# Two recurrence turns per loop body, and another order of instructions at a turn's boundary, in a hybrid decoder step

## What is computed

```python
def step(S, inp):
    r_t, w_t, k_t, v_t, a_t, b_t = inp
    sa = jnp.einsum('nhvk,nhk->nhv', S, a_t)
    S = S * w_t[:, :, None, :] + sa[..., None] * b_t[:, :, None, :] + v_t[..., None] * k_t[:, :, None, :]
    return S, jnp.einsum('nhvk,nhk->nhv', S, r_t)
...
mean = jnp.mean(y, axis=-1, keepdims=True)
var = jnp.mean(jnp.square(y - mean), axis=-1, keepdims=True)
y = ((y - mean) * lax.rsqrt(var + LNX_EPS)).reshape(n, t, A_WIDTH) * lnx_w + lnx_b
bonus = jnp.sum(r * k * r_k.astype(f32), axis=-1, keepdims=True) * v
y = (y + bonus.reshape(n, t, A_WIDTH)) * jax.nn.silu(za.astype(f32))
```

## Time and profile before

| what | value |
|---|---|
| runs | 3548.31, 3549.05, 3569.71 us, median 3549.05 us |
| profiled execution | 3559.79 us, span of the core 3558.3 us |
| granted clock of TensorE, mean | 0.945 |
| TensorE matmul | 92% of the span |
| TensorE weight load | 85% |
| VectorE | 48% |
| ScalarE | 30% |
| GpSimd | 11% |

### The profile page before, as it was taken

The page is one execution under the profiler, slowest core; times in us unless marked ns, Lnnn a source line. Parts: engine busy times, 40 slices in busy tenths (PEclk is TensorE's granted clock), DMA queues, the critical chain, the costliest instruction groups (busy, mean ns, idle before and its releaser), DMA issues. The chain is left out here.

```text
span 3558.3 us, 82556 instructions
## 1 busy us (share of the span) xinstructions
PE 3279.7 (92%) x33471; PEld 3028.9 (85%) x33471; DVE 1721.4 (48%) x2447; ACT 1054.2 (30%) x1680; POOL 395.8 (11%) x795
## 2 busy tenths in 40 slices
PE   3899999999997899999999999999999999996796
PEld 3798898898994889988988998998989998895796
DVE  3254454354443445655654654654654654563324
ACT  3232232332320322332332332432332332331222
POOL 2100100100001201110110110110110110111000
PEclk6899898998995999999999999999999999998898
DMA  2222323323313212221221221311221221221422
GB/s 86 71 79 72 125 73 91 119 60 103 106 36 108 71 53 56 74 55 45 75 62 38 74 63 43 80 51 49 75 62 49 64 62 50 61 61 42 150 75 97
DMA packets 368508, 255.10 MB, mean 72 GB/s; under 512 B 19412, under 2 KB 347600, under 8 KB 366288
## 3 DMA queue, kind: packets, MB, share of 16 engines
q1 hardware_dynamic: 342592, 184.18, 18.9%
q0 software_dynamic: 25600, 66.02, 5.8%
HBM read 212.69 MB, written 37.45 MB: 70 GB/s over the span
## 5 line engine op out<-in xcount | busy, mean ns | idle before, releaser
L363 PE MATMUL psum<-act_hi,w_hi 128*128 128x280 f32 (+3 forms) x5216 | 1613.2, 309 | 89.8 <-DVE w_lo L349 38.7
L365 PE MATMUL psum<-act_hi,w_lo 128*128 128x280 f32 (+3 forms) x5216 | 1539.9, 295 | 0.0
L364 PE MATMUL psum<-act_lo,w_hi 128*128 128x280 f32 (+3 forms) x5216 | 1539.1, 295 | 0.0
L363 PEld LDWEIGHTS psum<-act_hi,w_hi 128*128 128x128 f32 (+2 forms) x5216 | 999.6, 192 | 162.7 <-issue 107.0
L364 PEld LDWEIGHTS psum<-act_lo,w_hi 128*128 128x128 f32 (+2 forms) x5216 | 999.0, 192 | 6.0 <-issue 1.0
L365 PEld LDWEIGHTS psum<-act_hi,w_lo 128*128 128x128 f32 (+2 forms) x5216 | 998.3, 191 | 1.1
L349 DVE TENSOR_TENSOR w_lo<-raw,w_hi 128x1024 fp32r<-128x1024 f32 (+1 forms) x326 | 396.6, 1217 | 320.9 <-ACT w_hi L341 306.4
L341 ACT CAST w_hi<-raw 128x1024 fp32r<-128x1024 f32 (+1 forms) x326 | 340.1, 1043 | 87.4 <-DMA raw<-in_w_in_dram 36.5
L1937 PE MATMUL psum<-arena 64*64 64x64 f32 x9216 | 309.4, 219 | 6.6 <-DVE arena L1782 6.5
L1937 PEld LDWEIGHTS psum<-arena 64*64 64x64 f32 x9216 | 286.1, 134 | 32.9 <-issue 32.9
L1497 POOL DMA_DIRECT2D out_s_rwkv_dram<-arena x128 | 78.9, 624 | 1558.5 <-ACT arena L1639 1558.4
(11 more groups left out here) (312 smaller groups left out, 3513.8 us busy)
## 6 DMA issues: line engine op xcount, KB each, us to landing
raw<-in_w_in_dram SPq DMA_DIRECT2D x288, 512.0 KB, 4.6
arena<-in_state_gla_dram POOLq DMA_DIRECT2D x32, 512.0 KB, 5.3
out_s_gla_dram<-arena POOLq DMA_DIRECT2D x32, 512.0 KB, 3.3
raw<-in_w_out_dram SPq DMA_DIRECT2D x32, 512.0 KB, 4.5
ob_dram<-arena POOLq DMA_DIRECT2D x16, 280.0 KB, 3.1
arena<-ob_dram POOLq DMA_DIRECT2D x16, 280.0 KB, 5.8
m_dram<-arena POOLq DMA_DIRECT2D x16, 280.0 KB, 2.4
arena<-m_dram SPq DMA_DIRECT2D x4, 1120.0 KB, 12.2
```

What stands on the lines that cost most here:

```text
L363: pe.matmul(out, hi, act_hi[:, k, cols], start=(k == 0), stop=False)
L364: pe.matmul(out, hi, act_lo[:, k, cols], start=False, stop=False)
L365: mm = pe.matmul(out, lo, act_hi[:, k, cols], start=False, stop=(k == KT - 1))
```

## The change

All five edits are in stage D.

1. In the programs of GpSimd, ScalarE, VectorE and TensorE the loop has 7 passes of two turns, and turn 14 is written out behind it, ahead of turn 15. SyncE's loop is as before.
2. TensorE transposes the sample states after 16 steps of tile 3. ScalarE copies them between its two halves of tile 3's tanh.
3. Tile 4's tanh and its multiplication are taken in halves inside the doubling rounds: ScalarE's first half after its copy of round 1, VectorE's first half after its addition of round 2.
4. At the end of a turn TensorE takes the mean before the products of the sample states, and the variance 8 steps behind those, before the states are transposed. ScalarE splits tile 7 before it copies the results, and evacuates tile 6 and splits tile 8 behind the roots.
5. VectorE centres first, then splits tile 7 and computes the sample states; its split of tile 8 and its key shift come last in the turn.

```diff
-                with pool.Fori(0, LAST_TURN) as i:
-                    turn_of(i)
+                with pool.Fori(0, LAST_TURN // 2) as j:
+                    turn_of(2 * j)
+                    turn_of(2 * j + 1)
+                turn_of(LAST_TURN - 1)
                 turn_of(LAST_TURN, last=True)
...  (the same in the programs of ScalarE, VectorE and TensorE)
                 # ScalarE
-                    tanh_gate_of(3, tg)
-
+                    tanh_gate_of(3, tg, (0,))
                     act.wait_ge(s8_turned.sem, s8_turned.at(i, 1))
                     nc.scalar.copy(s8, bank[6].rearrange("p (s v) -> p s v", s=NSEQ)).then_inc(s8_ready.sem, 1)
                     act.wait_ge(s8_ready.sem, s8_ready.next(i))
+                    tanh_gate_of(3, tg, (1,))
...
                         to_sbuf(out, 6, inv_a)
-                    tanh_gate_of(4, tg)
+                        if n == 1:
+                            tanh_gate_of(4, tg, (0,))
+                    tanh_gate_of(4, tg, (1,))
...
                     tanh_gate_of(5, tg)
+                    if not last:
+                        pd.split_hi(act, i, mine, 7)
                     act.wait_ge(y_state.sem, y_state.at(i, 1))
...
-                    if not last:
-                        pd.split_hi(act, i, mine, 7)
-                        evacuate(act, i, mine, 6)
                     act.wait_ge(centred.sem, centred.at(i, 1))
                     nc.scalar.activation(e_t, y_t, ACT.Square).then_inc(squared.sem, 1)
...
                         act.wait_ge(signal.sem, signal.next(i))   # behind the two roots
+                    if not last:
+                        evacuate(act, i, mine, 6)
+                        pd.split_hi(act, i, mine, 8)
+                    states_out(0)
+                    states_out(1)
                     states_out(2)
...
                 # VectorE
+                        if n == 2:
+                            gate_second(0)
+                    gate_second(1)
                     if not last:
                         pd.split_lo(dve, i, mine, 6)
...
                     if not last:
-                        pd.split_lo(dve, i, mine, 8)
-                        shift_key(i, mine, 6)
+                        pd.split_lo(dve, i, mine, 7)
+                    dve.wait_ge(s8_done.sem, s8_done.at(i, 1))
...
                     dve.wait_ge(merged.sem, merged.next(i))
                     if not last:
+                        pd.split_lo(dve, i, mine, 8)
+                        shift_key(i, mine, 6)
                         mine.close()
...
                 # TensorE
-                    for _ in fill:
-                        pass
-
+                    for _ in range(4):
+                        next(fill)
                     pe.wait_ge(load_s8.sem, load_s8.at(i, 16 * NSEQ))
...
                     m.then_inc(s8_turned.sem, 1)
+                    for _ in fill:
+                        pass
...
                     m.then_inc(y_state.sem, 1)
-                    run(4)
+                    run(6)
+                    pe.wait_ge(y_ready.sem, y_ready.at(i, 1))
+                    pe.sem_inc(waited.sem, 1)
+                    head_sums(y_t, 4, mean_done)
                     for h in range(2):
...
                     m.then_inc(s8_done.sem, 1)
-                    run(10)
-                    pe.wait_ge(y_ready.sem, y_ready.at(i, 1))
-                    pe.sem_inc(waited.sem, 1)
-                    head_sums(y_t, 4, mean_done)
-                    run(20)
+                    run(8)
+                    pe.wait_ge(squared.sem, squared.at(i, 1))
+                    pe.sem_inc(waited.sem, 1)
+                    head_sums(e_t, 6, var_done)
+                    run(14)
                     pe.wait_ge(s8_next.sem, s8_next.at(i, 1))
                     pe.sem_inc(waited.sem, 1)
```

61 lines of the change are left out of this document (29 added, 32 removed).

## The result

The changed kernel takes 3570.05 us (median of 20 runs, 3562.03 to 3581.13), the kernel before, run beside it, 3561.62 us (median of 20, 3548.31 to 3571.05). The ratio is 1.0028 with a 95% interval of 1.0017 to 1.0039: about 10 us slower, where 9.5 us less was summed, and outside the range of 3514 to 3556. Part of that distance is the base: the three runs shown ahead of the prediction had a median of 3549.05, 12.6 us under what 20 runs give. From 3561.62 the same sum gives 3552. The other 18 us are the sum's own.

What follows compares the result with a forecast made beforehand. The prediction took TensorE as the bound, busy 126.33 of 130.14 us per turn. Savings of 15.8, 13.1, 0.9 and 2.4 us against costs of 7.5, 4.2 and 11.0 gave -9.5 us: 3540 us, range 3514 to 3556.

Steps and rivals of the forecast that it cites:

- the wait terms: All summed terms except the clock: branches, state copy, gate, tile 7, key reduction and ScalarE's refetch, -7.1 us together.
- the clock term: TensorE's 1.2 GHz stretches behind loop branches: 1.7 fewer expected with 6 of 14 branches left, -2.4 us.
- Two turns per body: At turn boundaries, 8 of TensorE's 14 taken branches go at 1.97 us each: -15.8 us.
- States early: TensorE's 0.82 us wait at the Gram products for the state copy goes in all 16 turns: -13.1 us.
- Gate in halves: Tile 5's 0.85 us wait moves to the chain's wait, making 1.29 us; only the last turn gains 0.9 us.
- the far bound: If the chain behind tile 4's gate had hidden slack, the gain would be 15 x 0.85 = 12.8 us.
- Tile 7's wait: New TensorE wait of about 0.5 us before tile 7 for ScalarE's evacuation of tile 6: 7.5 us more in 15 turns.
- The key reduction at straight boundaries: At a turn's head, a new TensorE wait of 0.6 us at 7 straight boundaries inside the loop: 4.2 us more.
- ScalarE's refetch at six branches: ScalarE's doubled body pays 3.0 us at its branch, leaving about 1.85 us at the key reduction, six times: 11.0 us more.
- rival 1: ScalarE's doubled loop stays resident, so the 11 us at its branches is not paid: 3529 us; chance 0.28.
- The branch itself: TensorE's six remaining taken branches at turn heads: no extra cost was counted for them.
- Rival 3: The clock drops at the merged 1.29 us chain wait; in all 15 turns that gives 3561 us; chance 0.12.

Runs made afterwards that it cites:

- e1: Kernel before with only the loop changed to two turns per body, every turn in the old order: 3548.94 us, ratio 0.9969.
- e5: Kernel before with only the sample states transposed early, after four fill steps, and copied between tile 3's tanh halves: 3548.57 us, ratio 0.9968.
- e6: Kernel before with only tile 4's gate taken in halves inside the doubling rounds: 3558.14 us, ratio 0.9999.
- e7: Kernel before with tile 4's gate in halves and the inverse's chain put ahead of the second gate half: 3553.74 us, ratio 0.9978.
- e12: Kernel before with three turns per body, early states, gate halves with the chain first, state products split by two fill steps: 3536.33 us, ratio 0.9947.
- e2: Changed kernel with one turn per loop body again, so only the order differs from the kernel before: 3596.47 us, ratio 1.0104.
- e4: Kernel before with SyncE held at the end of its pass until the last state copy, so the weight load runs over the branch: 3613.57 us, ratio 1.0154.
- e13: Changed kernel with VectorE's split of tile 8 and key shift put back ahead of its wait for the root: 3553.57 us, ratio 0.9978.
- e10: Changed kernel with its new order of the turn's end undone: 3548.03 us, ratio 0.9964 to the kernel before.
- e16: Kernel before with its 16 turns written out on the four computing engines, nothing else changed: 3538.96 us, ratio 0.9937.
- e15: Kernel before with early states, gate halves with the chain first, old end of turn, and all 16 turns written out: 3495.71 us, ratio 0.9825.
- e17: Changed kernel with its turns written out on the four computing engines, late split of tile 8 kept: 3528.75 us, ratio 0.9909 to the kernel before.

## Why the prediction was wrong, point by point

In short: the wait terms missed by 4 us only because two errors of about 12 us cancelled (a cost at TensorE's branch that was put at nothing, and one of ScalarE that did not come), and the clock term, put at -2.4 us, came out at about +15 us over all runs. The late weight load on the branch is behind the first and behind part of the second.

- **Two turns per body, -15.8 us.** Right. In e1 the branches go from 26.0 to 11.1 us, -14.9; with its new wait at the keys the sum was -11.6, and the kernel gained 0.31%, 11 us.
- **States early, -13.1 us.** Right: e5 gains 0.32%, 11 us, with nothing late behind it.
- **Gate in halves, nothing in 15 turns, the chain's wait at 1.29 us.** Right in mechanism (e6: 0.9999), and 1.53 us in size. The chain is not longer for it: from the start of the second half's tanh to TensorE's resumption it takes 6.27 us in both (1912.90 to 1919.17 before, 2175.78 to 2182.05 after). TensorE only comes to it about 1.1 us earlier and not 0.85. What the prediction called the far bound, 12.8 us, was to be had by another order (e7).
- **Tile 7's wait, 7.5 us.** It came, at 0.29 us and not 0.5: 4.3 us.
- **The key reduction at straight boundaries, 4.2 us.** Right: 0.6 us each, and none at branches.
- **ScalarE's refetch at six branches, 11.0 us.** Wrong, and rival 1 right about ScalarE, though not about the time (3529 us): it goes on 0.61 us after L386. The row with three turns a body (e12) has this term, at 2.93 us of ScalarE and some 1.2 us at TensorE.
- **The branch itself, put at nothing.** This is the step of the reasoning that failed. The prediction noted that VectorE "now does tile 8's split and the key shift last", and looked only at whether VectorE would be done in time for TensorE. It followed the load behind the split of tile 7 to its user, but not the one behind the split of tile 8 to where it would lie: on top of TensorE's code fetch. 3.8 us in place of 1.85, six times, is 12 us, and by chance nearly the 11 us that were counted for ScalarE. The same kind of delay is at VectorE's own branch, where the prediction expected about 3 us: in the records from its branch to its next instruction it is 2.7 to 3.1 us in e1 and 3.7 to 4.9 us in the changed kernel, off the path in both. So the wait terms come to -3.4 us where -7.1 were summed: right to 4 us, with one term replaced by another of its size.
- **Clock, -2.4 us.** Wrong in sign, and the larger part of the miss. The term counted only stretches behind branches, as 1.7 fewer, and took the late ones as unchanged; behind branches there were three more and late in the turn eight more. In the profile, 57.8 us more at 1.2 GHz at 1.6 us for each 3.4 us are 27 us; -3.4 and 27 make 24 of the 24.7 us measured over the 15 turns. Of the 27 us, 8 lie behind branches and 19 late in the turn. Over all runs the mean granted clock is 0.9431 against 0.9477; of 3565 us that is 16 us of full-speed time, or about 15 us at the measured price. With -3 us of waits that gives 12 us, where 10 were measured.

- **Slips in the working.** The nine plain turns last 130.07 to 130.70 us (the one of 130.70, from 2241.42 us on, was left out of the stated range), with a mean of 130.30, so the removed branch would be priced at 2.05 and not 1.97 us. The bounds of the two waits give 3531 to 3549 us, not 3526 to 3549. Neither changes the outcome.

Of the clock, part is explained: at the branch, 3 to 4 us without a matmul are followed by 1.2 GHz far more often than 1.9 us are (at 31 of the 34 branches of the changed kernel, e2 and e4, at three of 14 in the kernel before), and e13 gets 18 us back from a move whose wait was worth 13. Rival 3 had the right kind and the wrong place: the drops come at the head, behind a branch, and behind the state products, never at the merged wait. What is not explained is the late stretches, two thirds of the clock's share: why e1, e5 and e6 each keep a clock of 0.9467 to 0.9473, and together (e10) have 0.9426, with a time 10 us above the sum of their gains. In e16 eight turns of the same code and the same length in a row have a late stretch and the next has none. Filling waits elsewhere in a turn moved this block of small products in and out of stretches at 1.2 GHz in nearly every kernel of the table, and no run here says what decides it for one turn.

## What to carry to other kernels

When a step is moved to the end of a loop body, follow each transfer that it releases to the moment at which it will run: a megabyte of weights on top of a taken branch cost TensorE twice what the branch cost alone, although nobody was waiting for the weights. Put what a chain waits for ahead of what nobody waits for before adding capacity; and where a few microseconds of idle time per turn are at stake, writing the turns out (no branch, constants in the waits) gave 22 us here by itself (e16) and 28 to 30 us on top of the reorderings (e15), against some 11 and 8 us for the two reorderings that helped (e5, e7). A sum of removed waits is not yet a forecast for a TensorE-bound kernel: e7 got 8 us for 16.4 us of waits, because the clock took part of it. Count that term from several executions, not from one profile.

## What the runs showed of the hardware that was not expected

- A taken branch of TensorE costs 1.85 us with the DMA engines mostly free and 3.2 to 4.1 us when 1 MB of weights is on them (e1; e2, the changed kernel and e4). TensorE starts 1.8 to 2.1 us after the 16 KB packet on q8 has landed in every case, and the packet is not slower but starts up to 1.5 us behind the last matmul instead of 0.6 to 1.4 us ahead of its end.
- ScalarE's body of two turns passes its branch in 0.6 us, that of three in 2.93 us. The 8 KB code queue (q14) went from 34 to 76 packets with two turns a body, and 98 with three.
- Code that runs straight for 1900 us is fetched without a wait (e15: 2.5 us idle), next to 23% busy DMA engines.
- Waits whose target is computed from a loop counter put about 0.2 us between dependent VectorE operations in places where constants leave 0.04 us; over a chain of 16 us this was 1 us (15.9 against 14.9 us, loop turns and turn 15 of the kernel before).
- One stretch of 3.4 us at 1.2 GHz costs 1.5 to 1.6 us (128.0 and 129.6 us in e16, 127.8 and 129.3 in e17), and how many there are differs from kernel to kernel by more (3 to 78 us in 15 turns) than the waits that these kernels differ in.
